# Adding the squares of two chunks on the vector engine ahead of the mean-square matmuls, in one layer of a hybrid GLA and short-convolution diffusion backbone

## The reference

```python
def rmsnorm(x, g):
    xf = x.astype(jnp.float32)
    y = xf * lax.rsqrt(jnp.mean(xf * xf, axis=-1, keepdims=True) + EPS)
    return (y * g.astype(jnp.float32)).astype(x.dtype)

def swiglu(h, w1, w3, w2):
    return (jax.nn.silu(h @ w1) * (h @ w3)) @ w2

def block(x, mods, ...):
    h = rmsnorm(x, norm_ffn1) * (1.0 + m(1)) + m(0)
    x = x + 0.5 * m(2) * swiglu(h, w1_ffn1, w3_ffn1, w2_ffn1)
    h = rmsnorm(x, norm_mix) * (1.0 + m(4)) + m(3)
    mix, s_f, s_b = mixer(h, ...)            # chunked GLA, gated convolution, w_out
    x = x + m(5) * mix
    h = rmsnorm(x, norm_ffn2) * (1.0 + m(7)) + m(6)
    x = x + 0.5 * m(8) * swiglu(h, w1_ffn2, w3_ffn2, w2_ffn2)
    return x, s_f, s_b
```

## Time and profile before

| | us |
| --- | --- |
| Median of three runs | 1321.99 |
| The profiled execution, all cores | 1323.23 |
| Its span on the slowest core (core 4) | 1321.6 |
| PE busy in it | 1249.8 (95%) |
| DVE busy | 521.6 (39%) |
| ACT busy | 399.9 (30%) |
| POOL busy | 178.8 (14%) |
| Spans of the eight cores | 1310.7 to 1321.6 |

### The profile page before, as it was taken

The page is one execution under the profiler, slowest core; times in us unless marked ns, Lnnn a source line. Parts: engine busy times, 40 slices in busy tenths (PEclk is TensorE's granted clock), DMA queues, the critical chain, the costliest instruction groups (busy, mean ns, idle before and its releaser), DMA issues.

```text
span 1321.6 us, 19020 instructions; the slowest of 8 cores (1310.7 to 1321.6 us)
## 1 busy us (share of the span) xinstructions
PE 1249.8 (95%) x6648; PEld 573.2 (43%) x6648; DVE 521.6 (39%) x804; ACT 399.9 (30%) x647; POOL 178.8 (14%) x298
## 2 busy tenths in 40 slices
PE   2679999999999999989999999999999999999996
PEld 1234444444444444344444444444444444444444
DVE  2124134211233244466467667521243112432456
ACT  3265100111100245577545336621100111001344
POOL 3013100110001010110434322300001000000000
PEclk9989999999999999999999999999999999999999
DMA  9981734647734211010412322812313221020123
GB/s 176 220 195 33 128 58 71 96 65 115 111 62 69 53 68 53 0 33 0 97 18 51 94 70 59 137 23 45 57 28 59 38 32 33 1 48 1 64 64 128
DMA packets 35084, 91.05 MB, mean 69 GB/s; under 512 B 4016, under 2 KB 10672, under 8 KB 32816
## 3 DMA queue, kind: packets, MB, share of 16 engines
q0 software_dynamic: 21888, 62.11, 28.7%
q1 hardware_dynamic: 13104, 27.73, 6.3%
HBM read 137.24 MB, written 14.68 MB: 115 GB/s over the span
## 4 chain that ended last, share of the span: by engine, by line
PE 87%; DMA 5%; DVE 2%; ACT 2%; issue 2%; POOL 1%; DVEq 0%; ACTq 0%; POOLq 0%
PE ps L235 87%; DMA sb_arena<-w_ffn 4%; DVE sb_arena L263 1%; ACT sb_arena L248 1%; DMA sb_arena<-w_ada 1%; DVE sb_arena L252 1%; POOL sb_arena L232 1%; ACT L248 0%; POOL sb_arena L259 0%; PE ps L239 0%; POOL sb_arena L252 0%; DVEq L141 0%; ACTq L141 0%; DVEq L1207 0%; POOL sb_ea L269 0%
## 5 line engine op out<-in xcount | busy, mean ns | idle before, releaser
L235 PE MATMUL ps<-sb_arena 128*128 128x512 bf16 (+4 forms) x5840 | 1198.6, 366 | 25.8 <-DMA sb_arena<-w_ffn 8.3
L235 PEld LDWEIGHTS ps<-sb_arena 128*128 128x128 bf16 (+2 forms) x5840 | 536.7, 98 | 676.9 <-issue 69.9
L248 ACT ACTIVATE sb_arena<-ps 128x512 f32<-128x512 f32 (+3 forms) x281 | 166.1, 599 | 701.4 <-PE ps L235 700.3
L252 DVE TENSOR_TENSOR sb_arena<-sb_arena,ps 128x512 bf16<-128x512 f32 (+1 forms) x208 | 143.0, 688 | 481.1 <-PE ps L235 429.7
L263 DVE SCALAR_TENSOR_TENSOR sb_arena<-ps,sb_der,sb_arena 128x512 f32<-128x512 f32 (+1 forms) x200 | 145.2, 729 | 153.3 <-PE ps L235 153.3
L248 ACT ACTIVATE sb_arena<-sb_arena 128x512 bf16<-128x512 f32 (+4 forms) x193 | 123.5, 660 | 77.8 <-DVE sb_arena L263 63.0
L232 POOL DMA_DIRECT2D sb_arena<-w_ffn x88 | 47.1, 544 | 418.2 <-PE ps L235 388.2
L252 DVE TENSOR_TENSOR sb_arena<-sb_arena 128x512 f32<-128x512 f32 (+1 forms) x98 | 66.2, 717 | 55.1 <-ACT sb_arena L248 54.4
L259 POOL TENSOR_SCALAR sb_arena<-sb_arena,sb_der,sb_modT 128x512 bf16<-128x512 f32 x44 | 40.8, 928 | 267.2 <-DVE sb_arena L252 240.5
L263 DVE SCALAR_TENSOR_TENSOR sb_arena<-sb_arena,sb_vec 128x512 f32<-128x512 f32 (+1 forms) x72 | 53.2, 758 | 23.3 <-ACT sb_arena L248 13.4
L248 ACT ACTIVATE sb_arena<-sb_arena,sb_modT,sb_der 128x512 bf16<-128x512 f32 x48 | 39.0, 813 | 58.7 <-DVE sb_arena L252 44.8
(11 more groups left out here) (39 smaller groups left out, 158.5 us busy)
## 6 DMA issues: line engine op xcount, KB each, us to landing
sb_arena<-w_ffn POOLq DMA_DIRECT2D x44, 512.0 KB, 8.6
sb_arena<-w_ada POOLq DMA_DIRECT2D x36, 512.0 KB, 9.1
sb_arena<-w_ffn POOLq DMA_DIRECT2D x44, 256.0 KB, 9.4
sb_arena<-x SPq DMA_DIRECT2D x8, 1024.0 KB, 12.9
y<-sb_arena SPq DMA_DIRECT2D x24, 256.0 KB, 2.5
xspill<-sb_arena SPq DMA_DIRECT2D x4, 1024.0 KB, 4.0
sb_arena<-xspill SPq DMA_DIRECT2D x4, 1024.0 KB, 6.6
sb_arena<-w_cv POOLq DMA_DIRECT2D x12, 256.0 KB, 7.7
```

The lines of the kernel that those rows point to most:

```text
L235: return P.add("pe", lambda e: e.matmul(out, lhsT, rhs, start=start, stop=stop), reads=flat(reads), writes=flat(writes))
L248: return P.add("act", lambda e: e.activation(out=out, in_=in_, func=func, **kw), reads=flat(reads), writes=flat(writes))
L252: return P.add(eng, lambda e: e.tensor_tensor(out=out, in0=in0, in1=in1, op=op), reads=flat(reads), writes=flat(writes))
```

## The change

Two neighbouring chunks are now squared into f32 tiles, and DVE adds the two into one bf16 tile. The ones-matrix matmuls of a norm are four instead of eight. `square` keeps the addition back as a closure in `adds`, and emits it at the next call of `square`, which stands behind the next unit's DVE instruction, or at `add_pairs(0)`. There are two pairs of f32 tiles (`SQF`, 8 KB), and the squares of a pair wait until the addition that read these tiles is done. The room is taken from the squares (four tiles instead of eight) and from the ring at `TMP`, which has two tiles instead of four. All norms are changed that way but the first one of block 0, which keeps eight squares and eight matmuls, and the last block's halves.

For the first norm of blocks 1 to 3 the list of slices gets longer by one: four of squares, one for the last addition, an empty one, `stats` as one slice instead of two, and eight of `app`.

```diff
-        SQ, TMP, RSTD = 180 * KB, 188 * KB, 196 * KB
+        SQ, SQF, TMP, RSTD = 180 * KB, 184 * KB, 192 * KB, 196 * KB
...
+        adds = []
+
+        def add_pairs(keep):
+            while len(adds) > keep:
+                adds.pop(0)()
+
         def square(st, blk, kc):
 
-            st[kc] = P.alloc("sq%d" % kc, SQ + kc * KB, KB)
-            act(bf(SQ + kc * KB, 512), xv(kc, blk), AF.Square, [t_x[kc][blk]], [st[kc]])
-
-        def norm_slices(blk, apply, done=None):
+            add_pairs(0)
+            i = kc // 2
+            o = SQF + (i % 2) * 4 * KB + (kc % 2) * 2 * KB
+            t = P.alloc("sqf%d" % (kc % 2), o, 2 * KB)
+            act(f32(o, 512), xv(kc, blk), AF.Square, [t_x[kc][blk]], [t])
+            if kc % 2 == 0:
+                st["even"] = t
+                return
+            even = st["even"]
+
+            def add():
+                st[i] = P.alloc("sq%d" % i, SQ + i * KB, KB)
+                tt("dve", bf(SQ + i * KB, 512), f32(o - 2 * KB, 512), f32(o, 512), ALU.add, [even, t], [st[i]])
+
+            adds.append(add)
+
+        def norm_slices(blk, apply, done=None, paired=True):
...
-            def stats(k0, n):
-                for kc in range(k0, k0 + n):
-                    mm(ps[:, 7, :], onesB[:], bf(SQ + kc * KB, 512), kc == 0, kc == 7, [t_ones, st["sq"][kc]], [t_ps[7]])
-                if k0 + n == 8:
...
+            def stats():
+                add_pairs(0)
+                for kc in range(n):
+                    mm(ps[:, 7, :], onesB[:], bf(SQ + kc * KB, 512), kc == 0, kc == n - 1, [t_ones, st["sq"][kc]], [t_ps[7]])
...
             if done is None:
-                out += [(lambda k0=k0: squares(k0, 2)) for k0 in (0, 2, 4, 6)]
-                out += [lambda: stats(0, 4), lambda: stats(4, 4)]
-            else:
-                out += [lambda: stats(0, 8)]
+                out += [(lambda k0=k0: squares(k0)) for k0 in (0, 2, 4, 6)]
+                if paired:
+                    out += [lambda: add_pairs(0), lambda: None]
+            out += [stats]
             out += [(lambda kc=kc: app(kc)) for kc in range(8)]
...
-                i = nrm["t"] % 4
+                i = nrm["t"] % 2
...
-        for s in norm_slices(0, pre_apply):
+        for s in norm_slices(0, pre_apply, None, False):
             s()
...
                         F.down(16, 6, d, blk, nb)
                         square(sq, blk, d)
                         tick(1)
+                    add_pairs(0)
                     after_down(e[1], blk, sq)
...
                 square(sq, blk, d)
                 tick(2)
+            add_pairs(0)
             later(blk, norm6(blk, sq))
```

More of the change, by code:

```diff
@@ L335, in norm_slices, with squares @@
             st = {"sq": {} if done is None else done}
-            def squares(k0, n):
-                for kc in range(k0, k0 + n):
-                    square(st["sq"], blk, kc)
-            def stats(k0, n):
-                for kc in range(k0, k0 + n):
-                    mm(ps[:, 7, :], onesB[:], bf(SQ + kc * KB, 512), kc == 0, kc == 7, [t_ones, st["sq"][kc]], [t_ps[7]])
-                if k0 + n == 8:
[L345 to L348, removed]
+            n = 4 if paired else 8
+            def squares(k0):
+                for kc in range(k0, k0 + 2):
+                    if paired:
+                        square(st["sq"], blk, kc)
+                    else:
+                        st["sq"][kc] = P.alloc("sq%d" % kc, SQ + kc * KB, KB)
+                        act(bf(SQ + kc * KB, 512), xv(kc, blk), AF.Square, [t_x[kc][blk]], [st["sq"][kc]])
+            def stats():
+                add_pairs(0)
+                for kc in range(n):
+                    mm(ps[:, 7, :], onesB[:], bf(SQ + kc * KB, 512), kc == 0, kc == n - 1, [t_ones, st["sq"][kc]], [t_ps[7]])
+                r = f32(RSTD + sl * 2 * KB, 512)
+                st["r"] = P.alloc("rstd%d" % sl, RSTD + sl * 2 * KB, 2 * KB)
+                act(r, ps[:, 7, :], AF.Ln, [t_ps[7]], [st["r"]], scale=1.0 / D, bias=EPS)
+                act(r, r, AF.Exp, [st["r"]], [st["r"]], scale=-0.5)
             def app(kc):
```

## The result

The changed kernel takes 1330.62 us, the median of four runs (1329.43 to 1331.99), against 1321.89 us for the kernel before, measured again beside it: a ratio of 1.0065, 95% interval 1.0052 to 1.0078. That is 8.7 us slower where 4.3 were forecast. On another chip the same two kernels gave 1.0072 (1.006 to 1.0085). Medians here are over all runs of a kernel; the ratios leave out disturbed runs, in which the cores of a die show a lower granted clock and a longer time, and decide where the two differ. The profiled execution took 1330.82 us; the spans of its cores are 1325.2 to 1329.3 us, where those of before were 1310.7 to 1321.6.

What follows compares the result with a forecast made beforehand. PE, busy 95% of the span, was taken as the bound. Blocks 2 and 3 +5.2, block 1 +1.6, projection +2.2 and down units -4.7 gave +4.3 on the median 1321.99: 1326.3 us, range 1315 to 1331.

Steps and rivals of the forecast that it cites:

- Removed, 12.1 us: PE: 14 norms lose four matmuls each at 0.216 us, 12.1 us in all, the gain if all is hidden.
- Blocks 2 and 3, +2.6 each: First norms of blocks 2 and 3: PE stalls 3.5 us for late h tiles, less 0.86 saved; +5.2 for both.
- the chain of ten steps: Starts of blocks 2 and 3: steps from the end of `stats` to the last h tile, 16.1 us later.
- Above, +2.6 and a lower clock: First norms of blocks 2 and 3: upper edge of the estimate, the stall's +2.6 each with a lower PE clock added.
- rival 4: PE loses its clock after two stalls of 3.5 us, 1.7 us each on top: 1329.7 us, chance 0.17.
- the main case: Whole kernel: the summed terms, +4.3 us to 1326.3 us, own range 1324.6 to 1328.5, chance 0.45.
- Block 1, +1.6: First norm of block 1: last h tile at 84.9 instead of 83.4, +1.6 us, between -0.9 and +3.
- Projection, +2.2: Output projection: block 2's burst +1.6, blocks 3 and 0 +0.2 each, block 1 +0.2; between -3.4 and +5.
- 1.68 + four pairs 5.5 + 7 units 4.6 + additions 2.4 + 0.83 + 0.69 = 15.7: Output projection, blocks 3 and 0: DVE-bound time from one `stats` to the next, 15.7 us against 15.54 before.
- Down units, -4.7: Seven norms of the down units: -0.86 each, plus 1.3 for two loops sharing DVE; between -6 and -2.5.
- Rivals: 1 and 2: 1: all is hidden, 1309.9 us, chance 0.08. 2: the start of a block doesn't stall, 1316.9 us, chance 0.12.
- Rival 3: The later `stats` costs, the ring of two doesn't: 1319.8 to 1323 us, about no change, chance 0.18.

Runs made afterwards that it cites:

- the filled kernel: The changed kernel plus ten unread ones-matrix matmuls in the first up unit of each of blocks 2 and 3: 1332.21 us, ratio 1.0059 to the kernel before.

## Why the prediction was right in its sign and half in its size

- **Removed, 12.1 us:** right in count (56) and rate. PE's busy time fell by 4.5 only, mostly because at 1.2 GHz a matmul is busy for twice as long: core 4 of before ran at that level for 30.9 us in all, core 0 of after for 43.9, which is some 6.5 us of the 7.6.
- **Blocks 2 and 3, +2.6 each:** the chain of ten steps came out (last tile E + 15.98 for 16.1), and so did its price: +2.60 in the filled kernel, a delay of 3.46 (forecast 3.5) less 0.86. The split was right too: late `stats` with four tiles 2.04 (forecast 1.8), the ring of two the rest. **The step that failed is the last one:** "Above, +2.6 and a lower clock" was put at the edge of the case and given to rival 4 with 0.17, so the sum had nothing for the clock where 1.7 us each were lost, 3.3 of the 4.4 us by which the forecast was short. The argument against it, "the stalls are broken by matmuls", is refuted: five matmuls ahead of the 1.46 us of idle time and two between it and the 1.16 us did not keep the clock on any core. Rival 4's price of 1.7 us each was right; the main case and rival 4 together hold at these places. That rival 4's sum, 1329.7, is so near to the measured 1330.62 is in part luck: the projection and the down units were 1.2 and 1.3 us dearer than forecast on core 0, and the rest of the span gave 0.6 back.
- **Block 1, +1.6:** +1.6 on core 0, in part by luck. The forecast was a last tile 1.5 us later and nothing for the clock; measured are 1.1 us and 0.5 us of a longer stretch at 1.2 GHz, and the eight cores scatter from +0.5 to +2.7.
- **Projection, +2.2:** measured +3.4. The burst of block 2 was right (+1.61 for +1.6). The step "1.68 + four pairs 5.5 + 7 units 4.6 + additions 2.4 + 0.83 + 0.69 = 15.7" gave too little: 16.12. Three DVE instructions in that stream, an addition among them, end after 2.09 us beside POOL, where three without POOL took 1.89; which member of the sum holds the rest of the 0.4 was not parted. The up units behind it cost +0.6 where 1.0 less 0.86 was forecast; the interval of those units grew by 1.4 us, from 10.66 to 12.06. The ring alone makes 0.87 of that (0.88 with bf16 tiles), and the rest goes when the additions are short.
- **Down units, -4.7:** in part. On all eight cores the first norm gave 0.86, the second 0.1 (forecast 0.16), the fourth 0.86, and in the second SwiGLU 0.86, 0.26 (forecast 0.26) and 0.46 (forecast 0.86); at the last the fourth matmul waits 0.24 us for the last addition, so its cover was too short. That the second came out is in part luck, since 0.17 of its cost is the ring of two, which the forecast did not charge there. The third norm scatters between -1.9 and +2.6 us over the cores, and no price for it can be read: a wait of PE for DVE of 2.8 us, which before has too, follows it, and a stretch at 1.2 GHz behind that.
- **Rivals:** 1 and 2 fell with the stalls at 111.08 and 112.88. Rival 3 said that the late `stats` costs and the ring doesn't: the late `stats` is real (a stall of 2.04 each), but the ring costs as well, at the starts and behind the projection. Of DVE beside POOL the trace shows the multiplication of 105.84 at 1.00 us, begun within POOL's of 105.53, and 0.69 alone. The Trainium skill, "SBUF — State Buffer", section "Who interferes with whom", has the one that comes second wait until the other's instruction has ended. The trace agrees in kind, not in size: POOL's still had 0.46 us to run, and the multiplication lost 0.31.

## What to carry over

Before work is moved off the busiest engine, count what the edit does to the slot in which the dependent chain starts: here `stats` one slot later in a list cost 8.7 us by the ratios, against 12.1 us that all 56 matmuls could give at most. Putting it right (with tiles half as wide, which also freed room for the ring) turned +8.7 us into -8. Price a new stall of TensorE with the clock behind it, not by its idle time alone. And when an addition is put onto an engine that is already busy in that stage, look at what its inputs' type does to its length before giving room to the wider one.

## What the runs showed of the hardware that was not expected

- A stall in two pieces (1.46 and 1.16 us, with two matmuls between them and five before) came with 3.4 us at 1.2 GHz on eight cores of eight, at both places. Stalls of 1.56 and 0.16 us came with it at block 3 on four cores of eight, and at block 2 on none (in the kernel with bf16 tiles and a ring of four, 1.55 and 0.16 us, on none at either). Filled with matmuls whose result nobody reads (0.17 and 0.30 us of idle time left), on none.
- More matmuls made a kernel no slower, and at these places faster: 20 extra ones, 4.3 us of work, and PE gains 2.8 to 3.2 us over the two starts on all eight cores.
- An addition of two 128x512 tiles on DVE takes 0.44 us from bf16 and 0.69 us from f32; the square on ACT took the same with either output (0.63 us).
